# Cross-attention of a decoder step: three steps per token tile, sample queries spread by DMA, a sample's value products in four column groups

## The chip, the cores and the metric

The kernel runs on one core of a Trainium2 chip. The metric is the time of one execution on the device in microseconds; before the change the median of three runs is 2789.72 us (2788.94 to 2790.52).

## The reference

One layer of a decoder, in fp32, for a prompt of 1024 tokens and for 8 samples of one new token each: half-step SwiGLU, a token mixer (chunked gating beside an RWKV-7 scan), cross-attention into 256 memory tokens, half-step SwiGLU, final norm. The change is in the cross-attention alone:

```python
def cross_attn(h, mk, mv, w_q, w_o):
    bsz, t, _ = h.shape
    q = (h @ w_q).reshape(bsz, t, XA_HEADS, XA_HEAD_DIM)          # 4 heads of 256
    s = jnp.einsum('bthd,bmhd->bhtm', q, mk).astype(jnp.float32) * (XA_HEAD_DIM ** -0.5)
    p = jax.nn.softmax(s, axis=-1).astype(h.dtype)
    o = jnp.einsum('bhtm,bmhd->bthd', p, mv.astype(h.dtype)).reshape(bsz, t, D_MODEL)
    return (o @ w_o).astype(h.dtype)
```

The prompt has one memory (its keys and values are computed in the kernel). Each of the 8 samples has its own cached keys and values, 1 MB each, which are read from DRAM.

## The kernel before

Activations lie transposed in SBUF: x, qT and the like are [128, 8, 1032], with 1024 prompt tokens and the 8 samples as the last columns. Weights stream through four slots: SyncE loads raw pieces (line 335), GpSimd splits each into a high and a low part (lines 355 and 360), TensorE makes three products of a weight piece and 344 tokens (lines 382 to 384), and VectorE evacuates. All engines have their program written out by hand, and wait for one another by semaphores; what stands first in an engine's program is done first.

The attention lies between the projection xaq (it leaves qT) and the projection xao (it reads o_hi and o_lo, the two parts of the attention's output). `att_tensor`, `att_scalar` and `att_vector` hold the programs of TensorE, ScalarE and VectorE. Each goes through turns n = 0 to 8, with one tile of 128 prompt tokens each:

- scores of tile n into PSUM banks 0 and 1 (line 1739, n < 8); maxima (line 1877) and scaling (1880) on VectorE; exponentials with their sums on ScalarE (1826); reciprocal (1885) and normalisation (1886) on VectorE, into prob;
- in the next turn, for tile n - 1: eight transposes of prob into banks 2 and 3 (line 1760), copies to probT on ScalarE (1840), value products into banks 4 and 5 (1770), then o_hi on ScalarE (1845) and o_lo on VectorE (1914). On TensorE the value products stand right behind the transposes, and on ScalarE the copies to probT behind the exponentials of tile n.

The samples' work is threaded through the same turns. In turns 0 to 3, two samples each: TensorE spreads one query over all partitions by products of a broadcast column of qT with the identity (`att_query_pe`, line 1749, banks 6 and 7), and VectorE multiplies it with the sample's cached keys and sums, eight instructions a sample (`dots`, line 1863), into s_smp. In turn 4 the scores are transposed (1786), the sample softmax runs on 32 rows (1893 to 1898 and 1831), and the probabilities are transposed back (1795). In turn 5 they are spread into pT_smp, zero but for one sample's columns (1902 to 1905). In turns 5 to 8, two samples each: eight value products of 8 columns and 256 moving ones (line 1803), all writing rows 0 to 7 of banks 6 and 7. At the end o_rows is copied (1849 and 1919), transposed (1814), and becomes the last 8 columns of o_hi and o_lo (1851, 1921). The first product with xa_o waits for that.

SyncE's program holds, behind the weights of xaq, the loads of the 8 cached keys (`cache_loads`, line 1730) into two buffers, each behind the dot products that free its buffer, then those of the 8 cached values into the same two buffers, each behind the value products of the sample two before, then the weights of xao. GpSimd does nothing in the attention until the first piece of xa_o is there. An fp32 product shows in the trace as two records.

## Time and profile before

| | before |
|---|---|
| median of 3 runs | 2789.72 us |
| the profiled execution | 2790.14 us |
| its span (first to last instruction) | 2788.1 us |
| TensorE busy in the span | 2635.7 us (95%) |
| VectorE / ScalarE / GpSimd busy | 39% / 18% / 39% |
| attention, 1773.8 to 1921.7 us: TensorE / VectorE / ScalarE busy | 121.0 / 63.6 / 34.3 us of 147.9 |
| mean granted TensorE clock, whole span / attention | 0.965 / 0.91 of full speed |

A profile is one execution. Busy is the time in which an engine's instructions run; an idle engine costs time only where the chain that ended last passes through its wait. The granted clock is that of TensorE: 1.00 is 2.4 GHz and 0.50 is 1.2 GHz, and a value between them is a mean over a stretch with both. In a timeline, instructions of one line that follow one another are merged into one row with their count; the bracket gives the idle time of the engine before it and what released it.

### The profile page before, as it was taken

What the parts mean: (1) busy time and instruction counts of PE and PEld (TensorE: products, weight loads), DVE (VectorE), ACT (ScalarE), POOL (GpSimd) and SP (SyncE); (2) the same over time, 40 slices, a digit from 0 to 9 for tenths busy, and PEclk for the clock granted to TensorE, in tenths of its full rate; (3) what the DMA queues carried; (4) which work ended last, traced back from release to release, by engine and by line L of the source; (5) the groups of instructions that cost most, each with busy time, mean ns of one, the idle gap of its engine ahead of it and who ended that gap; (6) DMA issues with size and microseconds to landing.
All of it is one profiled execution on the core that took longest, in us unless ns stands there. A gap on an engine that the chain in (4) does not pass through costs nothing.

```text
span 2788.1 us, 50576 instructions
## 1 busy us (share of the span) xinstructions
PE 2635.7 (95%) x20619; PEld 2518.1 (90%) x20619; DVE 1086.5 (39%) x1850; ACT 515.0 (18%) x1035; POOL 1098.5 (39%) x866
## 2 busy tenths in 40 slices
PE   5999999999999998899978989879999999999998
PEld 5999999999999996789954989867999999999997
DVE  6332133223452674655445531442543213321333
ACT  4110011001221214322233240121211001100102
POOL 3444444444454441222214464002444444444442
PEclk8999999999999999899976999989999999999999
DMA  3111111111132110000023133123111111111111
GB/s 111 49 45 45 49 45 45 49 45 45 42 110 64 38 53 20 4 3 3 3 72 106 45 117 110 61 90 106 53 46 45 45 49 45 45 49 46 45 42 72
DMA packets 220704, 150.57 MB, mean 54 GB/s; under 512 B 10831, under 2 KB 211113, under 8 KB 219946
## 3 DMA queue, kind: packets, MB, share of 16 engines
q1 hardware_dynamic: 217530, 132.72, 15.9%
q10 hardware_dynamic: 2576, 16.11, 1.5%
q8 instruction: 89, 1.46, 0.2%
q14 instruction: 29, 0.24, 0.0%
q0 software_dynamic: 480, 0.05, 0.0%
HBM read 134.80 MB, written 14.04 MB: 53 GB/s over the span
## 4 chain that ended last, share of the span: by engine, by line
PE 92%; DVE 4%; ACT 2%; issue 1%; DMA 0%; POOL 0%; SPq 0%; DVEq 0%; ACTq 0%; POOLq 0%
PE bank L382 25%; PE bank L384 25%; PE bank L383 25%; PE bank L1020 1%; PE bank L1048 1%; PE bank L1770 1%; PE bank L1035 1%; PE bank L1739 1%; PE bank L1803 1%; PE bank L1064 1%; PE bank L1068 1%; PE bank L1089 1%; PE bank L1100 1%; PE bank L995 1%; PE bank L1079 1%
## 5 line engine op out<-in xcount | busy, mean ns | idle before, releaser
L355 POOL TENSOR_TENSOR w_hi<-raw,cst 128x512 fp32r<-128x512 f32 (+1 forms) x366 | 464.3, 1268 | 1238.7 <-PE bank L384 1067.5
L382 PE MATMUL bank<-h_hi,w_lo 128*128 128x344 f32 (+1 forms) x2856 | 915.3, 320 | 8.9 <-issue 7.5
L384 PE MATMUL bank<-h_hi,w_hi 128*128 128x344 f32 (+1 forms) x2856 | 913.1, 320 | 0.0
L383 PE MATMUL bank<-h_lo,w_hi 128*128 128x344 f32 (+1 forms) x2856 | 912.5, 319 | 0.0
L382 PEld LDWEIGHTS bank<-h_hi,w_lo 128*128 128x128 f32 (+1 forms) x2856 | 535.9, 188 | 11.2 <-issue 9.2
L360 POOL TENSOR_TENSOR w_lo<-raw,w_hi 128x512 fp32r<-128x512 f32 (+1 forms) x398 | 519.5, 1305 | 64.6 <-ACT w_hi L352 34.8
L384 PEld LDWEIGHTS bank<-h_hi,w_hi 128*128 128x128 f32 (+1 forms) x2856 | 536.1, 188 | 1.2
L383 PEld LDWEIGHTS bank<-h_lo,w_hi 128*128 128x128 f32 (+1 forms) x2856 | 534.9, 187 | 1.7
L384 PE MATMUL bank<-hid_hi,w_hi 128*128 128x344 f32 x1056 | 337.3, 319 | 0.0
L382 PE MATMUL bank<-hid_hi,w_lo 128*128 128x344 f32 x1056 | 337.2, 319 | 0.0
L383 PE MATMUL bank<-hid_lo,w_hi 128*128 128x344 f32 x1056 | 337.1, 319 | 0.0
L458 DVE TENSOR_TENSOR tmp<-bank,rstd 128x344 f32<-128x344 f32 x132 | 68.2, 517 | 338.2 <-PE bank L384 338.2
L492 DVE SCALAR_TENSOR_TENSOR x<-bank,x 128x344 f32 x120 | 62.0, 517 | 353.6 <-PE bank L384 353.6
L434 ACT ACTIVATE gate_s<-gate_s 128x344 f32<-128x344 f32 x132 | 64.6, 492 | 729.6 <-DVE gate_s L452 729.6
L384 PEld LDWEIGHTS bank<-hid_hi,w_hi 128*128 128x128 f32 x1056 | 198.6, 188 | 0.0
L382 PEld LDWEIGHTS bank<-hid_hi,w_lo 128*128 128x128 f32 x1056 | 198.5, 188 | 0.0
L383 PEld LDWEIGHTS bank<-hid_lo,w_hi 128*128 128x128 f32 x1056 | 198.2, 188 | 0.0
L452 DVE TENSOR_TENSOR gate_s<-bank,rstd 128x344 f32<-128x344 f32 x132 | 67.8, 516 | 289.9 <-PE bank L384 289.9
L438 ACT ACTIVATE hid_hi<-tmp 128x344 f32 (+1 forms) x132 | 64.9, 492 | 474.9 <-DVE tmp L464 474.9
L1273 POOL TENSOR_TENSOR LoT<-LQ,cst 128x512 f32<-128x512 f32 x40 | 51.7, 1301 | 168.7 <-PE bank L1020 87.2
L469 DVE TENSOR_TENSOR hid_lo<-tmp,hid_hi 128x344 f32 (+1 forms) x132 | 110.5, 863 | 0.0
L464 DVE TENSOR_TENSOR tmp<-tmp,gate_s 128x344 f32<-128x344 f32 x132 | 97.0, 735 | 13.8
(306 smaller groups left out, 3094.9 us busy)
## 6 DMA issues: line engine op xcount, KB each, us to landing
raw<-in_ffn_gate SPq DMA_DIRECT2D x88, 256.0 KB, 2.8
raw<-in_ffn_up SPq DMA_DIRECT2D x88, 256.0 KB, 2.9
raw<-in_ffn_down SPq DMA_DIRECT2D x80, 256.0 KB, 2.8
raw<-in_w_in SPq DMA_DIRECT2D x44, 256.0 KB, 2.8
cache<-in_cache_mem_k SPq DMA_DIRECT2D x8, 1024.0 KB, 5.0
cache<-in_cache_mem_v SPq DMA_DIRECT2D x8, 1024.0 KB, 4.9
x_save<-x ACTq DMA_DIRECT2D x1, 4128.0 KB, 12.5
x<-x_save ACTq DMA_DIRECT2D x8, 516.0 KB, 6.7
```

Of the source, the lines that this page charges most:

```text
L355: nc.gpsimd.tensor_tensor(w_hi[part], raw[part], cst[:, C_ONE:C_ONE + 1, 0:ph["width"]].to_broadcast([P, nk, ph["width"]]), ALU.mult)\
L360: nc.gpsimd.tensor_tensor(w_lo[part], raw[part], w_hi[part].bitcast(F), ALU.subtract).then_inc(split_done[slot], 1)
L382: nc.tensor.matmul(out, b, hi, start=first, stop=False)
L383: nc.tensor.matmul(out, a, lo, start=False, stop=False)
L384: m = nc.tensor.matmul(out, a, hi, start=False, stop=last)
L434: nc.scalar.activation(gate_s[:, t, :], gate_s[:, t, :], ACT.Silu)\
L438: nc.scalar.activation(hi[:, ds(i, 1), tslice(t)], tmp[:, t:t + 1, :], ACT.Copy).then_inc(S("hid_hi"), 1)
L452: nc.vector.tensor_tensor(gate_s[:, t, :], bank[3 * sg + t][:, 0:344], rstd[:, t, :], ALU.mult).then_inc(evac[sg], 1)
L458: nc.vector.tensor_tensor(tmp[:, t, :], bank[3 * su + t][:, 0:344], rstd[:, t, :], ALU.mult).then_inc(evac[su], 1)
L464: nc.vector.tensor_tensor(tmp[:, t, :], tmp[:, t, :], gate_s[:, t, :], ALU.mult)\
L469: nc.vector.tensor_tensor(lo[:, ds(i, 1), tslice(t)], tmp[:, t:t + 1, :], hi[:, ds(i, 1), tslice(t)].bitcast(F), ALU.subtract).then_inc(S( ...
L492: nc.vector.scalar_tensor_tensor(out=xs, in0=bank[3 * st + t][:, 0:344].rearrange("p (a n) -> p a n", a=1), scalar=scale, in1=xs, op0=ALU. ...
```

## The change

The turns become 0 to 9 and a tile goes through three of them instead of two. In turn n TensorE makes the scores of tile n, the transposes of tile n - 1 (`att_turn_pe`) and the value products of tile n - 2 (`att_out_pe`); ScalarE and VectorE follow (probT of tile n - 1, o_hi and o_lo of tile n - 2).

The queries of the samples are transposed once, ahead of turn 0, into 8 rows (`att_query_pe`), copied to q_rows, stored to a DRAM scratch q_d, and read back per sample to all 128 partitions (`query_loads` on SyncE's queue, between the key loads) into one of two buffers q_rep, behind the dot products that free it. The dot products read q_rep and not PSUM. They move to turns 1 to 4, the sample softmax to turn 5, the value products of the samples to turns 6 to 9.

The value products of a sample write head h into rows 32h to 32h + 7 of bank 6, with the head as the inner loop. The bank is set to zero before, o_rows is one copy of [128, 256], and two transposes replace eight. GpSimd waits for all dot products before it splits xa_o, since q_rows and q_rep lie in the buffers of the split weights.

```diff
@@ buffers
-        o_rows = at("o_rows", [NS, D], arena_z + 16 * ROW + 16384)
+        o_rows = at("o_rows", [P, XD], arena_z + 16 * ROW + 16384)
+        q_rows = at("q_rows", [NS, D], arena_w + 8192)
+        q_rep = [at("q_rep0", [P, D], arena_w + 16384), at("q_rep1", [P, D], arena_w + 20480)]
@@ TensorE
-        def att_query_pe(pe, n):
-
-            pe.wait_ge(S("s_dot"), 8 * n)
+        def att_query_pe(pe):
             for k in range(KD):
-                m = nc.tensor.matmul(bank[6 + k // 4][:, (k % 4) * P:(k % 4 + 1) * P],
-                                     qT[:, k, SEQ + n:SEQ + n + 1].to_broadcast([P, P]), ident,
-                                     start=True, stop=True)
-            m.then_inc(S("q_bc"), 1)
+                m = nc.tensor.transpose(bank[6 + k // 4][0:NS, (k % 4) * P:(k % 4 + 1) * P],
+                                        qT[:, k, SEQ:T], ident)
+                if k % 4 == 3:
+                    m.then_inc(S("srow"), 1)
+
+        def query_loads(sp, n):
+            if n == 0:
+                sp.wait_ge(S("rows_ev"), 2)
+                sp.dma_start(q_d, q_rows[:, :]).then_inc(S("scratch_stored"), 16)
+                sp.wait_ge(S("scratch_stored"), 32)
+            if n >= 2:
+                sp.wait_ge(S("s_dot"), 8 * (n - 1))
+            sp.dma_start(q_rep[n % 2][:, :], q_d[n, :].partition_broadcast(P)).then_inc(q_in[n % 2], 16)
...
+        def att_sample_pe(pe, b):
+            pe.wait_ge(S("srow_v"), 5)
+            pe.wait_ge(cache_in[b % 2], 64 + 16 * (b // 2 + 1))
+            for m in (0, 1):
+                for h in range(XH):
+                    i = nc.tensor.matmul(
+                        bank[6][32 * h:32 * h + NS, 0:XD],
+                        pT_smp[m].rearrange("p b x -> p (b x)")[:, 32 * b + 8 * h:32 * b + 8 * h + NS],
+                        cache[b % 2][:, m, h * XD:(h + 1) * XD],
+                        start=b == 0 and m == 0, stop=b == NS - 1 and m == 1, skip_group_check=True)
+            i.then_inc(S("o_smp"), 1)
...
-            for n in range(9):
+            att_query_pe(pe)
+            for n in range(10):
                 if n < 8:
                     att_scores_pe(pe, n)
-                if n < 4:
-                    att_query_pe(pe, 2 * n)
-                if n == 4:
+                if n == 5:
                     pe.wait_ge(S("s_dot"), 64)
...
-                if n:
-                    att_out_pe(pe, n - 1)
-                if n < 4:
-                    att_query_pe(pe, 2 * n + 1)
-                if n == 4:
+                if 0 < n < 9:
+                    att_turn_pe(pe, n - 1)
+                if n > 1:
+                    att_out_pe(pe, n - 2)
+                if n == 5:
                     pe.wait_ge(S("srow_v"), 2)
...
-                for b in (2 * n - 10, 2 * n - 9) if n > 4 else ():
...
+                if n > 5:
+                    att_sample_pe(pe, 2 * n - 12)
+                    att_sample_pe(pe, 2 * n - 11)
...
-            for k in range(KD):
-                i = nc.tensor.transpose(bank[0][:, k * NS:(k + 1) * NS], o_rows[:, k * P:(k + 1) * P],
-                                        ident[0:NS, 0:NS])
+            for d in (0, 1):
+                i = nc.tensor.transpose(bank[0][:, d * P:(d + 1) * P], o_rows[:, d * P:(d + 1) * P], ident)
             i.then_inc(S("srow"), 1)
@@ ScalarE
...
+                if n > 1:
+                    m = n - 2
+                    c = slice(m * P, (m + 1) * P)
                     for g in (0, 1):
                         act.wait_ge(S("pv"), 2 * m + g + 1)
@@ VectorE
-                dve.wait_ge(S("q_bc"), n + 1)
+                dve.wait_ge(q_in[b], 16 * (n // 2 + 1))
...
-                            in1=bank[6 + h // 2][:, (h % 2) * 256:(h % 2) * 256 + 256],
+                            in1=q_rep[b][:, h * XD:(h + 1) * XD],
...
-                    if n < 4:
-                        dots(2 * n)
+                    if 0 < n < 5:
+                        dots(2 * n - 2)
...
-                    if n < 4:
-                        dots(2 * n + 1)
+                    if 0 < n < 5:
+                        dots(2 * n - 1)
...
+                        nc.vector.memset(bank[6][:, 0:XD], 0.0).then_inc(S("srow_v"), 1)
@@ SyncE
             for n in range(8):
                 cache_loads(sp, "k", n)
+                if n == 1:
+                    query_loads(sp, 0)
+                if n > 0:
+                    query_loads(sp, n)
@@ GpSimd
+                if ph is xao:
+                    g.wait_ge(S("s_dot"), 64)
                 split_weights(g, ph, high=ph not in (memk, memv))
```

## Rows read from the trace of the kernel before

**Rows 1.** The page, part 4: the chain that ended last, by engine.
```profile
PE 92%; DVE 4%; ACT 2%; issue 1%; DMA 0%; POOL 0%; SPq 0%; DVEq 0%; ACTq 0%; POOLq 0%
```

**Rows 2.** Stretches: length, busy PE, PEld, DVE, ACT, POOL, then clock, DMA, GB/s.
```profile
1773.77:1921.67 147.90, 120.95 (x716) 96.65 (x717) 63.55 (x194) 34.25 (x100) 8.23 (x7) 0.91 0.33 111
...
1816.60:1832.90 16.30, 13.64 (x91) 12.67 (x90) 10.78 (x39) 4.10 (x12) 0.00 (x0) 0.90 0.38 129
```

**Rows 3.** Timeline of TensorE, turns with dot products: start, us, line, count [idle before].
```profile
1786.62 4.80 PE L1739 MATMUL bank<-kT,qT 128*128 128x256 f32 x16
...
1816.62 3.62 PE L1739 MATMUL bank<-kT,qT 128*128 128x256 f32 x16
...
1825.82 5.44 PE L1770 MATMUL bank<-probT,v_n 128*128 128x128 f32 x32 [2.35 <-ACT probT L1840]
1831.09 1.95 PE L1749 MATMUL bank<-cst,qT 128*128 128x128 f32 x16
```

**Rows 4.** Timeline of TensorE, turns with value products of samples, and the end.
```profile
1892.65 1.04 PE L1760 MATMUL bank<-cst,prob 128*128 128x128 f32 x8
1896.40 3.81 PE L1770 MATMUL bank<-probT,v_n 128*128 128x128 f32 x32 [2.71 <-ACT probT L1840]
...
1912.32 7.07 PE L1803 MATMUL bank<-cache,pT_smp 128*8 128x256 f32 x32
...
1921.67 0.42 PE L382 MATMUL bank<-o_hi,w_lo 128*128 128x344 f32 x1 [0.85 <-DVE o_lo L1921]
```

**Rows 5.** Timeline of VectorE at the end of turn 3 and in turn 4.
```profile
1833.08 0.42 DVE L1863 SCALAR_TENSOR_TENSOR s_junk<-cache,bank 128x256 f32<-128x256 f32 x1 [4.90 <-PE bank L1749]
...
1836.67 0.08 DVE L1863 DVE_READ_ACCUMULATOR s_junk<-cache,bank 128x1 f32 x1
...
1837.87 1.41 DVE L1877 TENSOR_REDUCE att<-bank 128x2 f32<-128x512 f32 x2
1839.31 0.17 DVE L1880 TENSOR_SCALAR att<-att 128x4 f32<-128x4 f32 x1
...
1841.69 1.22 DVE L1886 TENSOR_TENSOR prob<-prob,att 128x1024 f32<-128x1024 f32 x1
...
1844.22 0.34 DVE L1898 TENSOR_SCALAR p_smp<-p_smp,s_row 32x256 f32<-32x256 f32 x1
```

**Rows 6.** Timeline of ScalarE in turn 3: four exponentials, then the copies.
```profile
1823.26 0.47 ACT L1826 ACTIVATE prob<-bank,att 128x256 f32<-128x256 f32 x1 [7.63 <-DVE att L1880]
...
1825.07 1.09 ACT L1840 ACTIVATE probT<-bank 128x512 f32<-128x512 f32 x2
```

**Rows 7.** TensorE products in column groups and quadrants, and two weight loads (min/median/max).
```profile
914.54 1.09 PE L708 MATMUL bank<-gwT,vn 128*64 128x128 f32 x16
...
1158.12 1.91 PE L995 MATMUL bank<-AR,BK 64*64 64x128 f32 x61
...
L708 PEld LDWEIGHTS bank<-gwT,vn x128: 132/137/137, 914.5 to 1016.9; 128*64 128x64 f32 x128
...
L1803 PEld LDWEIGHTS bank<-cache,pT_smp x128: 85/90/90, 1862.4 to 1918.8; 128*8 128x8 f32 x128
```

**Rows 8.** Transfers: size, median us to landing; a wait for a store; a busy stretch.
```profile
cache<-in_cache_mem_k SPq DMA_DIRECT2D x8, 1024.0 KB, 5.0
...
fin_g<-in_final_norm SPq DMA_DIRECT2D x1, 512.0 KB, 4.9
...
SPq L1429 <- DMA smp_d<-smp_n: 7.2, 1, 7.2
...
1785.00:1787.00 2.00, 2.00 (x10) 1.95 (x10) 0.14 (x1) 0.00 (x0) 0.00 (x0) 0.50 1.03 426
```

**Rows 9.** Timelines of SyncE issues and of GpSimd at the end of the attention.
```profile
1903.79 3.82 SPq L1730 DMA_DIRECT2D cache<-in_cache_mem_v  x2
...
1913.20 1.26 POOL L355 TENSOR_TENSOR w_hi<-raw,cst 128x512 fp32r<-128x512 f32 x1 [160.02 <-DMA raw<-in_xa_o]
1914.54 1.27 POOL L360 TENSOR_TENSOR w_lo<-raw,w_hi 128x512 fp32r<-128x512 f32 x1
```

More of the change, by code:

```diff
@@ L1771, in att_out_pe @@
                                                  v_n[:, m, h * XD + d * P:h * XD + (d + 1) * P],
-                                                 probT[b][:, 2 * h + m, :], start=m == 0, stop=m == 1)
+                                                 probT[n % 2][:, 2 * h + m, :], start=m == 0, stop=m == 1)
                 i.then_inc(S("pv"), 1)
+        def att_sample_pe(pe, b):
[9 more added lines that the diff above has]
+            i.then_inc(S("o_smp"), 1)
         def att_tensor(pe):
@@ L1797, in att_tensor, with sample_cols @@
                     i.then_inc(S("srow"), 1)
-                for b in (2 * n - 10, 2 * n - 9) if n > 4 else ():
-                    pe.wait_ge(S("srow_v"), 4)
-                    pe.wait_ge(cache_in[b % 2], 64 + 16 * (b // 2 + 1))
-                    for h in range(XH):
-                        for m in (0, 1):
-                            i = nc.tensor.matmul(
-                                bank[6 + h // 2][0:NS, (h % 2) * XD:(h % 2 + 1) * XD],
-                                pT_smp[m].rearrange("p b x -> p (b x)")[
-                                    :, 32 * b + 8 * h:32 * b + 8 * h + NS], cache[b % 2][:, m, h * XD:(h + 1) * XD],
-                                start=b == 0 and m == 0 and h % 2 == 0, stop=b == NS - 1 and m == 1,
-                                skip_group_check=True)
-                    i.then_inc(S("o_smp"), 1)
-            pe.wait_ge(S("o_rows"), 2)
-            pe.wait_ge(S("o_hi"), 16)
+                if n > 5:
+                    att_sample_pe(pe, 2 * n - 12)
+                    att_sample_pe(pe, 2 * n - 11)
+            pe.wait_ge(S("rows_ev"), 3)
             pe.wait_ge(S("exp"), 32)
-            for k in range(KD):
-                i = nc.tensor.transpose(bank[0][:, k * NS:(k + 1) * NS], o_rows[:, k * P:(k + 1) * P],
-                                        ident[0:NS, 0:NS])
+            for d in (0, 1):
+                i = nc.tensor.transpose(bank[0][:, d * P:(d + 1) * P], o_rows[:, d * P:(d + 1) * P], ident)
             i.then_inc(S("srow"), 1)
+        def sample_cols():
+            return bank[0][:, 0:256].rearrange("p (d h x) -> p h d x", d=2, h=XH)[:, :, :, 0:NS]
         def att_scalar(act):
-            for n in range(9):
+            act.wait_ge(S("srow"), 1)
+            nc.scalar.activation(q_rows[:, 0:512], bank[6][0:NS, :], ACT.Copy).then_inc(S("rows_ev"), 1)
+            for n in range(10):
                 if n < 8:
@@ L1870, in att_vector @@
                 dve.wait_ge(evac[j], xaq["mm1"][j])
-            for n in range(9):
+            dve.wait_ge(S("srow"), 2)
+            nc.vector.tensor_copy(q_rows[:, 512:D], bank[7][0:NS, :]).then_inc(S("rows_ev"), 1)
+            for n in range(10):
                 if n < 8:
@@ L1917, in att_vector @@
                             .then_inc(S("o_lo"), 1)
-            dve.wait_ge(S("o_smp"), 8)
-            nc.vector.tensor_copy(o_rows[:, 512:D], bank[7][0:NS, :]).then_inc(S("o_rows"), 1)
+                if n == 5:
+                    dve.wait_ge(S("srow"), 4)
+                    for m in (0, 1):
+                        nc.vector.tensor_copy(
+                            pT_smp[m][:, :, 0:32:8],
+                            bank[7][:, m * 32:m * 32 + 32].rearrange("p (b h) -> p b h", b=NS))\
+                            .then_inc(S("srow_v"), 1)
             dve.wait_ge(S("o_hi"), 17)
-            nc.vector.tensor_tensor(o_lo[:, :, SEQ:T], bank[0][:, 0:64].rearrange("p (k b) -> p k b", k=KD),
-                                    o_hi[:, :, SEQ:T].bitcast(F), ALU.subtract).then_inc(S("o_lo"), 1)
+            nc.vector.tensor_tensor(o_lo[:, :, SEQ:T].rearrange("p (h d) b -> p h d b", d=2), sample_cols(),
+                                    o_hi[:, :, SEQ:T].rearrange("p (h d) b -> p h d b", d=2).bitcast(F),
+                                    ALU.subtract).then_inc(S("o_lo"), 1)
         def blk_rows(n):
@@ L1979, in program @@
         smp_d = nc.dram_tensor("smp_d", (6, NS, BW), F, kind="Internal").ap()
+        q_d = nc.dram_tensor("q_d", (NS, D), F, kind="Internal").ap()
         smp_od = nc.dram_tensor("smp_od", (NS, BW), F, kind="Internal").ap()
```

39 lines of the change are left out of this document (16 added, 23 removed).

## The prediction

> **What bounds the kernel now.** The chain of work that ended last comes first: 92% of it is TensorE [rows 1], so a change counts where TensorE stands idle, or where it stops doing work that is taken away. Next, the table of stretches cut where one token tile's turn of the attention ends and the next begins [rows 2], and in it the timelines of the three engines [rows 3 to 6]. The attention runs from 1773.8 us (behind the last piece of qT) to 1921.67 us (the first product with xa_o, [rows 2, 4]): 147.9 us, of which TensorE works 121, and in which the kernel makes nine turns. There are two kinds.
>
> Turns 0 to 3 each hold two samples' dot products on VectorE. A turn lasts 16.3 us with 13.6 us of TensorE and 10.8 us of VectorE [rows 2]: nobody is busy all the time, the engines wait for one another. TensorE spreads a query (1.95 us with its tail, [rows 3]), VectorE takes its products, the score products of the next tile stand behind the spread, and the value products wait 2.35 us for probT [rows 3], which ScalarE makes only after the exponentials of the same turn.
>
> Turns 5 to 8 each hold the value products of two samples: 32 records in 7.07 us, one every 221 ns [rows 4]. In turns 5 to 7 there is again a wait for probT, of 2.71 us [rows 4].
>
> **The change, part by part.** I lay the new order out turn by turn, with durations from the rows, first with TensorE at full clock and no late transfer.
>
> *Query spread.* It removes eight groups of 16 records from TensorE, about 1.8 us each beside their neighbours (1.95 less the tail), 14.4 us. It adds eight transposes of eight columns in their place, once, ahead of the first scores: eight transposes take 1.04 us with the tail [rows 4], so 1.0. The copies into q_rows hide behind the scores of tile 0. Then SyncE stores q_d, waits for it, and reads it back 128-fold, 512 KB a sample. Behind that wait on SyncE's queue stand only k loads 2 to 7, and these must wait for the first dot products anyway. The nearest row for a broadcast is fin_g, 512 KB landed in 4.9 us [rows 8]. A store followed by a wait took 7.2 us in a stretch full of other transfers [rows 8]; the trace has no quiet store of this size, so I take 2 with 7.2 as the other end. The rows of query 0 are there at 1775.7 + 2 + 4.9 = 1782.6, or 1787.8 at worst; they are wanted at 1785.8. Nothing to 2 us; I take nothing.
>
> *Turns 0 and 1.* Scores take 3.62 us [rows 3]. Turn 0: 1.0 + 3.6 of TensorE, 0.1 + 0.9 for the second maximum and the scaling (half of 1.41, and 0.17, [rows 5]), 1.9 for four exponentials (1823.26 to 1825.07, and a little to start them, [rows 6]): scores of tile 1 start at 1781.2, against 1786.6 now [rows 3]. VectorE has their maxima at 1785.8, then dot products 0, normalisation and dot products 1. Eight dot products take 3.6 us (1833.08 to 1836.67); a normalisation takes 1.22 [rows 5], with the small reciprocal before it 1.35. That ends at 1794.35. Reading the query from SBUF and not from PSUM I cost at nothing either way.
>
> *Turns 2 to 4* are VectorE's: 1.6 (maxima, scaling) + 3.6 + 1.35 + 3.6 + 1.2 (o_lo, 1836.67 to 1837.87) = 11.35 us [rows 5]. TensorE needs only 3.6 + 0.95 + 3.75 = 8.3 us of it (scores, transposes, value products, [rows 3, 4]) and its waits for exponentials and probT fall inside, since the value products now belong to the tile before. So three turns are 34.05 us: 1828.4.
>
> *Turn 5* has the sample softmax. From the first maximum to the end of p_smp the rows give 1837.87 to 1844.56, 6.7 us [rows 5]; with its transposes 1835.4. The memsets and o_lo lie behind that beside TensorE's 8.3 us of turn 6.
>
> *Samples' value products.* Now all four heads of a sample write 8 rows in a column group of their own. Products with two column groups, 16 records, took 1.09 us with a tail of 0.2, some 64 ns each, where 128 columns otherwise take about 117 ns (32 records in 3.75 us): 1.8 times as fast [rows 4, 7]. In four quadrants 64 records took 2.0 us, 32 ns each, 3.7 times [rows 7]. Four column groups are not in the trace. From both sides: 7.07 us a pair of samples if they don't overlap, 3.9 at the ratio of two groups, 1.9 at that of four quadrants. I take 2.0, since the number of tiles is that of the last row.
> The Trainium skill ("TensorE: Matmul & The Clock Gate", Part 3) says that a weight load overlaps a running product only where the row groups differ, and here all use the same 128 rows. The trace disagrees: with two column groups on the same rows a record came every 64 ns while a weight load lasts 137 [rows 7]. By that rule 32 loads of 90 ns would make 2.9 us a pair.
>
> *Turns 6 to 9.* Turns 6 and 7: 8.3 + 2.0 each, 1856.0. Turn 8 has no scores: 4.7, then sample 4. V load 5 was issued at 1856.0 behind v4. 1 MB lands in 5.0 us, and while it moves the transfers run at 426 GB/s [rows 8], 2.5 us each; so v5 lands at 1862.3, and sample 5 ends at 1863.3. There v7 is issued, right behind v6, and lands at 1869.0. Turn 9 does value products to 1867.1, sample 6 to 1868.1 and sample 7 to 1870.0. Now two things end together. The tail from the last sample product to xa_o takes 2.3 us today (1919.39 to 1921.67, [rows 4]): 1872.4. And xa_o's first piece, issued behind v7: it reaches GpSimd 6.0 us after v7's issue today (1907.24 to 1913.20), and the split takes 2.6 [rows 9]; v7 lands 5.7 us after issue here and 4.9 there, so 1872.8. This is what comes last: a new wait of 0.4 us that replaces a larger one, and GpSimd's added wait for the dot products is long fulfilled by then.
>
> **The sum.** 1921.67 - 1872.8 = 48.9 us. From it I take three costs. (a) The clock: after idle stretches the records show 1.2 GHz for some us; scores took 4.80 where 3.62 is usual, value products 5.44 for 3.81 [rows 3, 4]. Tile 1's scores come after 2.8 idle us: 1.2. The scores of tile 6 come after several short waits: 1.6. In turns 2 to 4 TensorE has 3 us to spare, so this costs nothing there. (b) Loads: k (2.5 us of moving), then the query (about 2.2, as 512 KB in smaller pieces), land some 7.3 us after dot products free the buffer; the next use comes 6.55 us later in turn 2, twice, and 7.75 later in turns 3 and 4. 1.5. Together 4.3, leaving 44.6. The profiled execution took 2790.14 (span 2788.1 and 2.0 around it), so 2745.5; the median of the runs is 0.4 lower. I say 2746.
>
> **Rivals.**
> *The column groups don't overlap* (the change does not do what it says). For: no row with four; all read the same partitions. Against: two groups gave 1.8. Each of four turns grows by 5.07, less 0.6 and 0.9 us of waits for loads and 0.4 at the end which vanish: +18.4, so 2764. With the ratio of two groups (3.9 a pair) it is about +6: 2752. With every weight load bare (2.9), +2.6: 2748.
> *TensorE at 1.2 GHz much of the time.* For: now it idles 3 of 11.35 us in turns 2 to 4; the granted clock is already 0.90 in a turn with 2.35 us of idle [rows 2, 3]. Against: behind the idle 2.71 us of turn 7 the value products took the usual 3.81 [rows 4], and the idle stretches of turns 6 to 9 go away. At a mean of 0.8 in turns 6 to 9 (some 34 us of products) and at the first scores: +8 or 9, 2755.
> *Loads bound turns 2 to 4.* A turn can't be shorter than landing time + 3.6. At 9.5 us from issue to landing it costs 2 x 2.95 us in turn 2 and 1.75 in each of the next two, 9.4 and so 7.9 more than under (b): 2754. **Slower than before** comes out by this mechanism only: three turns must lose 45 us, so the pair of loads must take about 15 us longer than the 7.75 that fit, some 23 us, three times my estimate, for example if the 128-fold read of one 4 KB row went through few engines. fin_g speaks against it. It would give 2795.
>
> **How the numbers follow.** My forecast, 2740 to 2753 with the milder overlap cases in it: 0.70. No overlap, 2764: 0.12. Clock, 2755: 0.09. Loads, 2754: 0.07. Slower: 0.02. The range runs from 2739 (nothing of (a) and (b) lost, and the better overlap) to 2765, which takes in no overlap. A difference of 0.2%, 5.6 us, is about what can be told from no change here; every case but the last is beyond it. Faster 0.97, same 0.01, slower 0.02.
>
> **What would show it.** Turns 2 to 4 of 11.4 us, VectorE busy over 90% in them; no wait of TensorE for probT; the sample's 16 records within 1.0 us (3.5 would be no overlap); about 3.6 us from one score group to the transposes and 8.3 + 2 in turns 6 and 7; xa_o's first product near 1877. I am wrong if VectorE's dot products wait for q_rep for more than 2 us in all, if the granted clock in turns 6 and 7 is below 0.9, or if anything after the attention changes its length by more than 2 us.

## The result, and the profile after

The changed kernel takes 2743.47 us (median of 4 runs, 2740.64 to 2744.99) beside 2789.33 for the kernel before on the same chip: ratio 0.9834, 95% interval 0.9819 to 0.985. The forecast was 2746, within 2739 to 2765. The profiled execution took 2743.82 us, its span is 2741.8.

Stretches of the kernel after: length, busy PE, PEld, DVE, ACT, POOL, granted clock, DMA share, GB/s. The first is the whole attention, from the query transposes to the first product with xa_o; then turns 2 to 4, cut where VectorE begins a turn's maxima; then turns 6 to 9, cut where TensorE begins a turn.

```profile
1773.98:1876.91 102.93, 80.71 (x591) 68.96 (x591) 63.46 (x195) 34.90 (x102) 2.58 (x3) 0.93 0.56 195
...
1796.40:1808.20 11.80, 6.25 (x39) 5.36 (x38) 10.82 (x41) 3.88 (x12) 0.00 (x0) 0.94 0.84 287
1808.20:1820.70 12.50, 10.61 (x56) 9.91 (x56) 10.88 (x40) 3.99 (x12) 0.00 (x0) 0.79 0.71 257
1820.70:1832.30 11.60, 8.35 (x54) 7.53 (x55) 10.84 (x40) 3.88 (x12) 0.00 (x0) 0.93 0.66 227
...
1839.30:1849.24 9.94, 9.94 (x90) 8.28 (x89) 6.22 (x13) 5.04 (x15) 0.00 (x0) 1.00 0.01 2
1849.24:1859.18 9.94, 9.94 (x92) 8.29 (x88) 4.31 (x7) 3.99 (x12) 0.00 (x0) 1.00 0.55 213
1859.18:1867.92 8.74, 6.70 (x76) 5.23 (x72) 1.38 (x2) 2.28 (x4) 0.00 (x0) 1.00 0.77 274
1867.92:1877.00 9.08, 6.40 (x71) 4.65 (x67) 1.61 (x3) 1.80 (x4) 2.67 (x3) 1.00 0.95 315
```

The attention takes 102.93 us instead of 147.90 [rows 2], 45.0 less. TensorE's busy time in it falls from 120.95 to 80.71, and its idle time only from 26.95 to 22.22. Of the 40.2 us of busy time, about 34 are work that is gone: four times 5.16 for the samples' products (7.07 less 1.91) and eight query spreads of about 1.8, less the 0.9 of the new transposes. The other 6 or so are products that ran at half clock before and no longer do. To credit the third step with the 4.7 us of idle time alone would be misleading (second experiment). Turns 2 to 4 are now VectorE's: it is busy 87 to 93% of them. Turns 6 and 7 are TensorE's without a gap, and turns 8 and 9 have waits again, with the DMA queues 77 and 95% busy.

TensorE's timeline of the kernel after (start, duration, line, records; in brackets the idle time before and what ended it), the rows where time is lost and one clean turn:

```profile
1781.48 5.41 PE L1742 MATMUL bank<-kT,qT 128*128 128x256 f32 x16 [3.01 <-ACT prob L1842]
...
1808.34 6.28 PE L1781 MATMUL bank<-probT,v_n 128*128 128x128 f32 x32 [3.72 <-DVE o_lo L1928]
...
1839.30 3.72 PE L1742 MATMUL bank<-kT,qT 128*128 128x256 f32 x16
1842.86 1.04 PE L1769 MATMUL bank<-cst,prob 128*128 128x128 f32 x8
1843.73 3.74 PE L1781 MATMUL bank<-probT,v_n 128*128 128x128 f32 x32
1847.40 1.91 PE L1791 MATMUL bank<-cache,pT_smp 128*8 128x256 f32 x32
...
1864.43 1.05 PE L1791 MATMUL bank<-cache,pT_smp 128*8 128x256 f32 x16 [0.58 <-DMA cache<-in_cache_mem_v]
1866.94 1.05 PE L1791 MATMUL bank<-cache,pT_smp 128*8 128x256 f32 x16 [1.46 <-DMA cache<-in_cache_mem_v]
...
1873.42 1.05 PE L1791 MATMUL bank<-cache,pT_smp 128*8 128x256 f32 x16 [0.68 <-DMA cache<-in_cache_mem_v]
1874.97 0.44 PE L1826 MATMUL bank<-cst,o_rows 128*128 128x128 f32 x2 [0.50 <-ACT o_rows L1867]
1876.91 0.42 PE L384 MATMUL bank<-o_hi,w_lo 128*128 128x344 f32 x1 [1.50 <-POOL w_lo L362]
```

The pair of samples that took 7.07 us [rows 4] takes 1.91 (1847.40). The scores at 1839.30 to the samples at 1847.40 are one turn without a wait: where turns 5 to 7 of before had 2.71 us for probT [rows 4], nothing is left. What is left: cold products, that is products at 1.2 GHz, after 3 us of idleness (1781.48: 5.41 where 3.72 is usual), 2.7 us of waits for value loads, and the last row, where xa_o's first product waits for GpSimd's split.

The remainder of the kernel changed too. The first 6 us from xa_o's first product on, of the kernel before and then of the kernel after:

```profile
1921.67:1927.67 6.00, 6.00 (x28) 6.00 (x29) 0.00 (x0) 0.00 (x0) 1.77 (x2) 0.72 0.30 90
```

```profile
1876.91:1882.91 6.00, 6.00 (x38) 6.00 (x39) 0.00 (x0) 0.00 (x0) 5.84 (x5) 1.00 0.31 90
```

In 6 us, 38 products instead of 28 run, at a granted clock of 1.00 instead of 0.72: 10 products of 0.16 us, 1.6 us. From xa_o's first product to the end the span is 866.4 us before (2788.1 less 1921.67) and 864.9 after, the same 1.5. Span before to span after: 45.0 in the attention, 1.5 behind it, less 0.2 by which the attention starts later, 46.3.

### The profile page after: what moved, and what is told of

The parts are those of the page before. It is cut to its first block, busy times and chain, and to the rows that moved or that the text cites. A ratio compares the mean times of both kernels' runs of the same rounds, so it can differ in the third digit from the quotient of the medians.

```text
span 2741.8 us, 50335 instructions
## 1 busy us (share of the span) xinstructions
PE 2595.5 (95%) x20493; PEld 2491.2 (91%) x20493; DVE 1084.8 (40%) x1851; ACT 514.3 (19%) x1036; POOL 1098.4 (40%) x866
## 4 chain that ended last, share of the span: by engine, by line
PE 89%; DVE 4%; issue 3%; ACT 2%; DMA 1%; POOL 0%; SPq 0%; DVEq 0%; ACTq 0%; POOLq 0%
PE bank L384 25%; PE bank L386 25%; PE bank L385 25%; PE bank L1022 2%; PE bank L1050 1%; PE bank L1037 1%; PE bank L1066 1%; PE bank L1070 1%; DMA q_rep<-q_d 1%; PE bank L1091 1%; DVE s_junk L1881 1%; PE bank L1102 1%; PE bank L997 1%; PE bank L1093 1%; PE bank L1081 1%
```

## The experiments

My theory is that of the prediction: each of the three parts does what it says, and what is left over is VectorE's work, loads and the clock. The rivals differ in how much each part carries. Each part is taken back alone first; then the groups are made alone. The kernel before took 2790.33 us on the chip of these four, 2789.33 beside the changed kernel and 2789.18 and 2789.35 on the chips of the later ones, so what an edit costs is the difference of two gains, each over the kernel before on its own chip; the change's gain is 45.9. By its 95% interval such a gain is good to some 4.5 us either way, so a difference of two gains from different chips to about 6.

**The column groups taken back.** All heads of a sample write rows 0 to 7 again; the transposes and the two copies of before come back with it.

```diff
-            for m in (0, 1):
-                for h in range(XH):
+            for h in range(XH):
+                for m in (0, 1):
                     i = nc.tensor.matmul(
-                        bank[6][32 * h:32 * h + NS, 0:XD],
+                        bank[6 + h // 2][0:NS, (h % 2) * XD:(h % 2 + 1) * XD],
```

> The changed kernel, but with the samples' value products as before: all four heads into rows 0 to 7 of banks 6 and 7, 32 records of 221 ns a pair of samples, and o_rows copied and transposed as before. My theory (the products of the four groups overlap, and they lie on TensorE's path in turns 6 to 9): each pair takes 7.07 us again for the 1.84 that it takes in the changed kernel, 20.9 in all, less the waits for value loads in turns 8 and 9 (0.6, 1.5 and 0.7 us) which vanish: +18, so 2762 us. Rival: the samples' products fill time in which TensorE would wait for loads anyway; then less than +6, under 2750.

Measured: 2762.1 us (2759.1 to 2762.26), ratio 0.9896 (0.988 to 0.9913). Its TensorE timeline, two of its four pairs:

```profile
1846.81 7.07 PE L1791 MATMUL bank<-cache,pT_smp 128*8 128x256 f32 x32
...
1884.29 7.07 PE L1791 MATMUL bank<-cache,pT_smp 128*8 128x256 f32 x32
```

A gain of 28.2 instead of 45.9: the groups are worth 17.7 us in the full kernel. Four times 5.16 would be 20.6; some comes back because none of these products waits for a load any more. The rival without overlap gave 2764, with +18.4. My own rival, that these products only fill time in which TensorE would wait for loads (under 2750), is out.

**The third step taken back.** The value products, o_hi and o_lo go back to the turn of the transposes; query spread by DMA and groups stay.

```diff
-                if n > 1:
-                    att_out_pe(pe, n - 2)
+                if 0 < n < 9:
+                    att_out_pe(pe, n - 1)
```

> The changed kernel, but in two steps a tile: the value products, o_hi and o_lo of tile n - 1 stand in turn n, right behind its transposes and its copies to probT. My theory: the wait for probT comes back, 2.7 us in each of turns 6 and 7, some 4 in turn 5 (there ScalarE also makes the exponentials of the samples first), under 1 in each of turns 2 to 4 where VectorE is the bound: +9 to +13, so about 2754 us. Rival: VectorE and the loads bound the turns and the wait hides: +3 or less, under 2747. Other rival: the third step is the main part of the gain of 46 us: +20 or more.

Measured: 2762.88 us (2761.61 to 2763.83), ratio 0.9903 (0.9886 to 0.9919), so the third step is worth 18.4 us (45.9 less 27.5). I had expected 2754, +9 to +13; the result is nearer to the rival with +20, in which this step is the main part. Rows of its TensorE timeline, one of turn 3 and then from turn 5 on:

```profile
1813.79 3.81 PE L1781 MATMUL bank<-probT,v_n 128*128 128x128 f32 x32 [2.71 <-ACT probT L1855]
...
1840.15 5.41 PE L1781 MATMUL bank<-probT,v_n 128*128 128x128 f32 x32 [5.04 <-ACT probT L1855]
...
1853.04 5.44 PE L1781 MATMUL bank<-probT,v_n 128*128 128x128 f32 x32 [2.71 <-ACT probT L1855]
1858.40 1.91 PE L1791 MATMUL bank<-cache,pT_smp 128*8 128x256 f32 x32
...
1867.55 5.36 PE L1781 MATMUL bank<-probT,v_n 128*128 128x128 f32 x32 [2.71 <-ACT probT L1855]
...
1886.05 1.90 PE L1791 MATMUL bank<-cache,pT_smp 128*8 128x256 f32 x16 [3.36 <-DMA cache<-in_cache_mem_v]
```

The wait of 2.71 us for probT is back, and in turns 6 and 7 the value products behind it take 5.4 us instead of 3.74: there a wait of 2.7 us costs 4.4. The wait alone does not decide this. In turns 1 and 3 of this kernel the same 2.71 us were followed by products of 3.81 us (1813.79), and in the kernel before by 3.81 in turns 5 and 7 [rows 4], but by 5.44 in turn 6:

```profile
1876.73 5.44 PE L1770 MATMUL bank<-probT,v_n 128*128 128x128 f32 x32 [2.71 <-ACT probT L1840]
```

From scores 6 to scores 7 it is 14.5 us (1845.73 to 1860.25) instead of 9.94. TensorE's busy time in the attention is 87.3 us here and 80.7 in the full change, for the same products: 6.6 us of it is clock, 10.2 us more is idle, and 2.2 more are lost behind the attention, where the clock is 0.59 in the first 6 us. So the 4.7 us by which idle time shrank from before to after is not what the third step is worth. Without it TensorE idles 32.4 us (119.71 of attention less 87.3), 5.4 more than before: that is what the other two parts uncover, and the third step takes 10.2 away.

**The query spread taken back.** The samples' queries are spread by TensorE's products into banks 6 and 7, with the dot products in turns 1 to 4.

```diff
+                if 0 < n < 5:
+                    att_query_pe(pe, 2 * n - 2)
...
+                if 0 < n < 5:
+                    att_query_pe(pe, 2 * n - 1)
...
-                            in1=q_rep[b][:, h * XD:(h + 1) * XD],
+                            in1=bank[6 + h // 2][:, (h % 2) * 256:(h % 2) * 256 + 256],
```

> The changed kernel, but with each query spread by TensorE's products into banks 6 and 7 as before, the first of a turn behind the scores and the second behind the value products; no q_d and no q_rep. My theory: in turns 1 to 4 VectorE is the bound at 11.35 us with or without them, TensorE has 8.3 + 3.6 = 11.9 us of work, VectorE waits some 0.6 us a turn for the second query, and the waits for q_rep (1.6 us) and the transposes ahead (0.9) go away: 2742 to 2746 us, no difference to the changed kernel. Rival: the products taken from TensorE (14.4 us) are time gained: +12 or more, over 2755.

Measured: 2752.16 us (2749.47 to 2752.91), ratio 0.9861 (0.9845 to 0.9878). The gain falls by 7.7 us (45.9 less 38.2), so this part carries something, against my expectation. Its TensorE timeline:

```profile
1790.34 3.42 PE L1751 MATMUL bank<-cst,qT 128*128 128x128 f32 x16 [2.89 <-DVE s_junk L1883]
...
1809.58 2.05 PE L1751 MATMUL bank<-cst,qT 128*128 128x128 f32 x16 [0.31 <-DVE s_junk L1883]
...
1841.71 0.42 PE L1821 MATMUL bank<-cst,p_smp 32*128 32x32 f32 x2 [2.78 <-DVE p_smp L1918]
1842.06 6.56 PE L1742 MATMUL bank<-kT,qT 128*128 128x256 f32 x16
```

The products themselves find room beside VectorE's turns. What costs is that each spread must wait until VectorE has read the one before out of the same banks, and VectorE then waits for the spread: 6.4 us in six waits, 2.16 the longest, where it waits 1.6 us for q_rep in the full change. And the scores of tile 6 run at half clock (6.56 us, +2.8), as do the first products with xa_o (granted clock 0.51 over 6 us, +2.7 us from there to the end). Against that, the scores of tile 1 ran at full clock here (3.72 us from 1781.07, where the change has 5.41), which gives 1.7 us back, and the transposes ahead are gone, 0.8. The span is 8.7 us longer than that of the change (2750.5 and 2741.8): 4.8 are the longer waits of VectorE (6.4 less 1.6), of which 1.4 are a spread at half clock (3.42 us at 1790.34 for 2.05), and some 3.8 net are the other places where the clock fell; the rest is a later start and value loads. So 4 to 5 us are clock. Whether these come with the edit, or with the moment, these runs don't separate: the changed kernel itself, profiled twice, has its cold value products in turn 3 once and in turn 4 the other time (1808.34 and 1820.98).

**The groups alone, on the kernel before.**

```diff
@@ on the kernel before
-                                bank[6 + h // 2][0:NS, (h % 2) * XD:(h % 2 + 1) * XD],
+                                bank[6][32 * h:32 * h + NS, 0:XD],
```

> The kernel before, with the column groups alone: the samples' value products, o_rows and its transposes as in the changed kernel, everything else (two steps, queries by products, turns 0 to 8) as before. My theory: turns 5 to 7 lose 5.2 us each, and the end (from sample 5 to xa_o) goes from 14.5 to 9 us, where the last loads bind: -21, so 2768 us. Rival: the freed time turns into waits for value loads and for probT, and half of it or less is gained: 2779 or more.

Measured: 2772.06 us (2769.64 to 2774.13), ratio 0.9932 (0.9916 to 0.9949), 18.3 us gained where I expected 21. Its TensorE timeline, of the slowest of the four runs:

```profile
1872.24 6.76 PE L1770 MATMUL bank<-probT,v_n 128*128 128x128 f32 x32 [2.71 <-ACT probT L1842]
1878.93 1.91 PE L1803 MATMUL bank<-cache,pT_smp 128*8 128x256 f32 x32
...
1888.09 5.44 PE L1770 MATMUL bank<-probT,v_n 128*128 128x128 f32 x32 [2.71 <-ACT probT L1842]
```

Here is the loss on TensorE that the taken-back third step showed: of the three value products behind 2.71 us, two run cold, 4.6 us together, where the kernel before had one (1.6 us). So 3.0 us of the four times 5.16 go to the clock. The three parts taken back one by one give 17.7 + 18.4 + 7.7 = 43.8, near the whole of 45.9. The groups are worth the same, within the noise, with the other two parts and without them (17.7 and 18.3), and the third step is worth 19.9 beside the groups alone (38.2 less 18.3) and 18.4 in the full kernel. So the gains in time nearly add up, although the idle times do not. The third step and the query spread alone, on the kernel before, were not run. Of the third step's worth 8.8 us are clock: 6.6 in the attention and 2.2 behind it.

**Two groups instead of four.** Heads 0 and 1 write one group, 2 and 3 another.

```diff
-                for h in range(XH):
-                    i = nc.tensor.matmul(
-                        bank[6][32 * h:32 * h + NS, 0:XD],
+                for hh in (0, 1):
+                    for g in (0, 1):
+                        h = 2 * g + hh
+                        i = nc.tensor.matmul(
+                            bank[6][32 * g:32 * g + NS, hh * XD:(hh + 1) * XD],
```

> The changed kernel, but the four heads in two column groups: heads 0 and 1 in rows 0 to 7, heads 2 and 3 in rows 32 to 39 of bank 6 (512 columns), in turns; o_rows and its transposes are twice as wide. If the rate goes with the number of groups, as in the kernel before with two groups of 64 columns: 110 to 120 ns a record, 3.6 to 3.9 us for two samples, +6 us to the changed kernel less 1 of waits for loads: 2749. If two groups are already as fast as four (one limit for all): 1.84 us a pair, no difference but 0.4 us at the end.

Measured: 2747.18 us in one run, too few for a verdict on the time; the pair takes 3.63 us. A row of its TensorE timeline:

```profile
1846.00 3.63 PE L1793 MATMUL bank<-cache,pT_smp 128*8 128x256 f32 x32
```

With one, two and four groups a record comes every 221, 113 and 60 ns (7.07, 3.63 and 1.91 us over 32). Two groups are 1.95 times as fast as one, four are 3.70 times.

**The order of the heads.** The four heads side by side, or a head's two halves behind one another (two records in the same group):

```diff
-            for m in (0, 1):
-                for h in range(XH):
+            for h in range(XH):
+                for m in (0, 1):
```

> The changed kernel, but the two products of a head (both halves of the memory) follow one another, so that four records in a row go to one column group. Theory A (each group has its own stream, a record starts as soon as its group is free): a waiting record holds up those behind it, so up to four records of 221 ns are in a row before the next group starts, and about two groups overlap at most: 16 records take 2 to 3.5 us where they take 0.92 now. Theory B (order doesn't matter, the records are queued by group): 0.92 us as now.

Measured: 2746.07 us in one run; a pair takes 1.93 us instead of 1.91. The order of the heads does nothing to the products, whose rows are what this run was for. Theory A had wanted 2 to 3.5 us for 16 records, and it is out (1.07 here). Of the mechanism, this says only that four groups are kept filled even when neighbours share one.

**A second transfer of each query.** SyncE loads every query twice, the second time into a weight slot that is free, and VectorE waits for both.

```diff
             sp.dma_start(q_rep[n % 2][:, :], q_d[n, :].partition_broadcast(P)).then_inc(q_in[n % 2], 16)
+            sp.dma_start(raw[:, 2 * (n % 2):2 * (n % 2) + 2, :, :].rearrange("p a b c -> p (a b c)"),
+                         q_d[n, :].partition_broadcast(P)).then_inc(q_in[n % 2], 16)
```

> The changed kernel, but every query is read from q_d a second time, 512 KB more a sample, into the idle raw weight buffers, and the dot products wait for both. My theory of the loads (a turn with two samples moves 2 x 2.5 us of keys and 2 x 2.2 us of queries through the 16 engines, against 11.4 to 12.5 us a turn): 13.8 us of moving a turn now bound turns 2 to 4, each by 2 to 2.5 us longer, and turn 2 more: +7 to +9, so 2752 us. Rival: the broadcast costs only latency, and twice the bytes are hidden: under +2.

Measured: 2746.71 us (2745.52 to 2748.03), ratio 0.985 (0.9833 to 0.9866), 3.4 us of the gain lost. That is within the noise of a difference between two chips, though each of its four runs is slower than each of the change's; the waits point the same way. What VectorE waits for, total, times and longest, in this kernel and then in the kernel after:

```profile
DVE s_junk L1883 <- DMA raw<-q_d: 4.3, 3, 2.8
```

```profile
DVE s_junk L1881 <- DMA q_rep<-q_d: 1.6, 4, 0.8
```

The wait grew by 2.7 us for 4 MB more (by 3.4 over the other profile of the change, with 0.9), so loads stand at the edge of setting turns 2 to 4: neither free (I had a rival under +2) nor the bound (+7 to 9). Each load landed 6.2 and 7.6 us after its issue, and the key loads beside them no later than before (4.9 us, against 6.1 and 5.2 in two profiles of the change). Landing times are no measure of the queue's room by themselves.

**The first idle stretch kept warm.** TensorE makes three useless products of 512 columns in its first 3 us wait; their results are never read.

```diff
+                if n == 0:
+                    pe.wait_ge(S("rows_ev"), 2)
+                    for _ in range(3):
+                        nc.tensor.matmul(bank[7][:, 0:512], kT[:, 0, 0:P], kT[:, 0:2, :].rearrange("p k n -> p (k n)"),
+                                         start=True, stop=True)
```

> The changed kernel with three products of 512 columns more, of no use, into the free bank 7 behind the scores of tile 0, where TensorE stands idle for 3.0 us; the output is the same. If the granted clock is what makes tile 1's scores 5.41 us and not 3.62: the idle stretch is filled, they take 3.6, and VectorE's turns start 1.8 us earlier: 2741.7 us. Rival: the scores are not on the path of turn 1 (VectorE would wait for the first query rows), or the clock falls all the same: no difference.

Measured: 2742.82 us (2740.83 to 2747.22), ratio 0.9833 (0.9817 to 0.985), no difference from the change that these runs can tell. Its TensorE timeline:

```profile
1779.61 2.74 PE L1808 MATMUL bank<-kT 128*128 128x512 f32 x6
1782.78 3.72 PE L1742 MATMUL bank<-kT,qT 128*128 128x256 f32 x16 [0.43 <-ACT prob L1847]
...
1789.51 5.41 PE L1742 MATMUL bank<-kT,qT 128*128 128x256 f32 x16 [2.13 <-ACT prob L1847]
...
1838.53 5.41 PE L1742 MATMUL bank<-kT,qT 128*128 128x256 f32 x16
```

This profile is of the slowest of the four runs, 4.4 us above their median. It does what was meant: the scores of tile 1 take 3.72 us instead of 5.41. VectorE's turn 2 begins 20.7 us after the attention's start (1796.02 less 1775.28), in the change 22.4 (1796.40 less 1773.98). The scores of tile 2 are now cold (1789.51, behind a wait of 2.13 that left the same scores warm in the change), but VectorE had other work until 1796.02, so they cost nothing. The 1.7 us are lost later: the scores of tile 6 (1838.53) are cold and were warm there, and the waits for value loads in turns 8 and 9 are 3.6 us instead of 2.7. The attention takes 103.46 us in this run, against 102.93. So in this run the gain was given back. How it went in the three faster runs no trace shows, and a gain of 1.8 us, as expected, is less than these medians could tell from none.

**The waits for loads removed.** Three edits of the transfers, none of the arithmetic. (1) Five q_rep buffers: SyncE spreads samples 0 to 4 right behind the store. (2) The values of samples 4 to 7 are loaded into the place of qT as soon as its last scores are done. (3) xa_o's first four pieces are loaded behind v1, and GpSimd splits them while the attention runs.

```diff
-            if n >= 2:
-                sp.wait_ge(S("s_dot"), 8 * (n - 1))
+            if n >= 5:
+                sp.wait_ge(S("s_dot"), 8 * (n - 4))
...
+            if name == "v" and n >= 4:
+                sp.wait_ge(S("score"), 16)
+                sp.wait_ge(S("s_dot"), 64)
+                sp.dma_start(cache_late[n - 4][:, :, :],
...
             for n in range(8):
                 cache_loads(sp, "v", n)
-            load_weights(sp, xao)
+                if n == 1:
+                    load_weights(sp, xao, 0)
+            load_weights(sp, xao, 1)
```

> The changed kernel with its loads moved, the arithmetic untouched. Five buffers for the spread queries in place of two (samples 0 to 4 are spread right behind the store, 5 to 7 behind k2 to k4); the value loads of samples 4 to 7 go to the place of the prompt's queries, which is free once the scores of tile 7 are done, and no longer wait for a buffer; the first four pieces of xa_o's weights are loaded behind v1, and GpSimd may split them at once. Theory A (after the change the path still holds waits for loads: 1.6 us on VectorE for the spread queries, 2.7 us on TensorE for v5 to v7, 1.5 us of xa_o's first product for the split): these 5.8 us go, less what the k loads lose because five spread queries now stand ahead of k2; 2738 to 2740. Theory B (the DMA queues are full in this stage, and what is loaded earlier only makes something else late): VectorE now waits for k2 and k3, 2743 or more. Warm clock after the attention as in the changed kernel.

**The changed kernel once more**, for the comparison on one chip:

> The changed kernel itself on the same chip as the two above, for their difference: 2743.5, within 0.1%.

**And the normalisation on ScalarE**, on top of the loads:

```diff
-                    nc.vector.tensor_tensor(prob[b][:, :, :], prob[b][:, :, :],
-                                            att[:, b, 2, :].unsqueeze(2).to_broadcast([P, XH, NMEM]),
-                                            ALU.mult).then_inc(S("pnorm"), 1)
@@ ScalarE
+                    for h in range(XH):
+                        nc.scalar.activation(prob[n % 2][:, h, :], prob[n % 2][:, h, :], ACT.Copy,
+                                             scale=att[:, n % 2, 2, h:h + 1]).then_inc(S("pnorm"), 1)
```

> e8_early_loads with one more edit: the probabilities are normalised on ScalarE (four copies with a scale, one for each head) in place of VectorE's one product of 128x1024, so that a turn of VectorE, which sets turns 1 to 4, is shorter by that product. If VectorE's own work sets the turns (its busy time 10.8 of 11.6 us in them), turns 1 to 4 lose about 1.2 us each, 4.8 in all: 2734 to 2736. If the landing of k loads already sets them (512 KB and 512 KB per 10.5 us is what the queues moved at 0.84 busy), VectorE waits for DMA instead and less than 2 us come: 2737 to 2740.

Measured in five runs each: the change again 2743.91 us (2742.6 to 2745.37); with the loads moved 2739.6 (2736.3 to 2740.97), ratio to the kernel before 0.9821 (0.9808 to 0.9834); with the normalisation as well 2733.72 (2733.55 to 2735.85), ratio 0.9803 (0.9789 to 0.9816). Every run of the last is below every run of the second, and these are below every run of the change on this chip. TensorE's timeline at the end of the attention, of the kernel with the loads moved:

```profile
1860.55 1.91 PE L1816 MATMUL bank<-cache_late,pT_smp 128*8 128x256 f32 x32
1862.39 3.84 PE L1802 MATMUL bank<-probT,v_n 128*128 128x128 f32 x32
1866.16 1.91 PE L1816 MATMUL bank<-cache_late,pT_smp 128*8 128x256 f32 x32
1868.58 0.44 PE L1851 MATMUL bank<-cst,o_rows 128*128 128x128 f32 x2 [0.50 <-ACT o_rows L1892]
1869.59 0.42 PE L397 MATMUL bank<-o_hi,w_lo 128*128 128x344 f32 x1 [0.57 <-DVE o_lo L1965]
```

No row waits for a DMA, and xa_o's first product waits 0.57 us for o_lo instead of 1.50 for GpSimd. Its attention takes 96.90 us (1772.69 to 1869.59) instead of 102.93, 6.0 less where 5.8 was the sum of the three waits. The medians say 4.3: the profiled run is the fastest of the five, 3.3 us under their median, so what it shows of the attention may be its best case.

With the normalisation moved, VectorE's turns 3, 4 and 5 begin at 1806.82, 1817.02 and 1827.22, 10.2 us apart, against 11.33 (1806.43, 1817.76, 1829.09) in the kernel with the loads alone: 1.1 us a turn for a product of 1.25. In turn 2 it waits once for a key load. What VectorE waits for in this kernel:

```profile
DVE s_junk L1911 <- DMA cache<-in_cache_mem_k: 1.4, 1, 1.4
```

So VectorE's own work did set the turns, and the loads are now the next bound. (What I wrote on loads before the run was miscounted: a turn moves two keys of 1 MB and two queries of 512 KB, not 1 MB in all.) The median is 5.9 us below the kernel with the loads moved, where 4.8 was expected, and 10.2 below the change. Against the change the profile says the same: an attention of 93.05 us (1773.90 to 1866.95), 9.9 less than 102.93.

## Why the prediction was right

**The sum.** The forecast for the profiled execution was 2745.5, with xa_o's first product at 1877.1 after the 4.3 us of costs. It came at 1876.91, with a start 0.2 us later. So the length of the attention was forecast to 0.4 us; the other 1.5 us lie behind it. Part of this closeness is luck: tile 6's scores began 1.0 us later than the forecast with its costs and the later start would have them (1838.3), and then the 1.6 us of clock that I put on these scores did not come. The figure of 2746 for the median was also rounded up: 2745.5 less 0.4 is 2745.1.

**Query spread: held.** The store was issued at 1775.86 and the first spread 1.8 us later; I took 2, with 7.2 as the other end. VectorE's first dot products did not wait. A dot product from SBUF takes 0.42 us, as from PSUM. The transfers ran beside VectorE's turns nearly as laid out, and taking this part back cost 7.7 us.

**Turns 0 and 1: right, cost (a) too small there.** Tile 1's scores began at 1781.48 (forecast 1781.2). They took 5.41 us: 1.8 lost to the clock, where I had 1.2. Turn 2 of VectorE began at 1796.40 instead of 1794.35, which is this and the later start.

**Turns 2 to 4: right.** 35.9 us to 1832.31, forecast 34.05 plus 1.5 of cost (b). VectorE waited 0.39, 0.82, 0.21 and 0.17 us for q_rep, 1.6 in all; with five buffers the turns are 11.33 us, where I had laid out 11.35. VectorE was busy over 90% only in two of the three turns, 87% in turn 3. That TensorE's cold products cost nothing there is right too: the value products at 1808.34 took 6.28 us, the clock was 0.79 in that turn, and its 1.6 us of VectorE's idle time hold 1.0 of wait for the loads, while the other 0.6 are there in turn 2 too.

**Turn 5: right but for cost (a).** From 1832.31 to tile 6's scores at 1839.30 it is 7.0 us, as forecast (1835.4 less 1828.4). The 1.6 us that I put on these scores for the clock did not come: 3.72 us. They did come in two experiments (6.56 and 5.41). The sum of both terms of (a) was 2.8, measured 1.8 in this run; where the cold stretch falls is not to be had from the profile of before, and it moves between two executions of the changed kernel too.

**Four groups: right by the row, wrong by the rule.** 1.91 us a pair, taken as 2.0 from the row of four quadrants [rows 7]. The groups of instructions of the kernel after, by line and shape, have the samples' products and their weight loads (busy time, mean ns of one, idle time before):

```profile
L1791 PE MATMUL bank<-cache,pT_smp 128*8 128x256 f32 x128 | 8.0, 379 | 2.7 <-DMA cache<-in_cache_mem_v 2.7
...
L1791 PEld LDWEIGHTS bank<-cache,pT_smp 128*8 128x8 f32 x128 | 3.0, 89 | 6.3 <-issue 3.8
```

A record takes 379 ns by itself, and one ends every 60. The 379 alone say little, since they are the same in the kernel before, where one ends every 221; it is the interval that shows several under way at once. The weight loads of 89 ns on the same 128 rows must then overlap products of other column groups, and one another. The Trainium skill ("TensorE: Matmul & The Clock Gate", Part 3) wants different row groups for that, and the trace disagrees here also with four groups. By that rule the estimate was 2.9 us a pair (32 loads of 90 ns). Another page of the Trainium skill, "TensorEngine Tiling (Array Packing)" ("When to Use Tiling"), gives column tiling a factor of four for a stationary side of 32 columns; here, with 8, 3.7 was measured (7.07 over 1.91), and 1.95 for two groups.

**Turns 6 to 9: two small misses that cancel.** Turns 6 and 7 took 9.94 us each, not 10.3. In turns 8 and 9, loads were waited for 0.58, 1.46 and 0.68 us, 2.7 in all; I had 0.6 and 0.9 for v5 and v7, and none for v4. The term mis-sized is the landing of the two value loads that follow one another: v4 took 5.8 us from its issue, where I had 5.0 [rows 8], and v5 7.5 where I had 6.3. The loads v6 and v7 took 4.9 and 5.2.

**The last wait: the right one.** I named GpSimd's split of xa_o's first piece as what comes last. The last row waits for it. With the pieces loaded earlier, the way from the last sample product to xa_o is 1.5 us instead of 2.4, so it cost 0.9 us and not 0.4.

**After the attention: missed.** I forecast no change there and got 1.5 us. Its cause is in the granted clock of xa_o's first 6 us, 0.72 before and 1.00 after. The experiments show the sign is not safe: it was 0.59 with two steps, 0.51 with the query by products and 0.72 with the warm products, and the time behind the attention follows it (867.1, 867.6 and 866.5 us against 864.9). So it does in all thirteen profiles: seven with 1.00 need 864.9 us there, four with 0.72 (the kernel before, one group, the groups alone, the warm products) 866.4 or 866.5. What decides the clock at that point stays open.

**The rivals.** No overlap was priced at 2764, and the kernel that has none took 2762.1. Loads as the bound of turns 2 to 4: a second query transfer cost 3.4 us, less than half of the 7 to 9 that it would cost if they were, so they were close but not there. The clock as a large loss did not happen: it was 1.00 in turns 6 to 9. But what I held against it was thin: I named the 3.81 us behind the wait of turn 7, and turn 6 of the same profile has 5.44 behind the same wait. The experiments make the clock the least understood term: of what the taken-back third step and query spread cost, 8.8 and 4 to 5 us were clock.

## What to carry to other kernels

Where several small products each fill a few columns of the array, put them into column groups of their own; the gain is nearly the number of groups. Do not price a part of a change by the net fall of an engine's idle time: work that is taken off an engine uncovers waits behind it, and an idle stretch of 2.7 us on TensorE cost 4.4 where the products behind it ran at half clock, as they did after some of these waits and not after others. A pipelining step that the idle times credit with 5 us was worth 18. Take each part back alone; here the gains so found nearly add up to the whole. When one bound falls, look for the loads that were issued late because nothing asked for them sooner: freed buffers and idle space moved them earlier, and this gave another 4.3 us.

## What was not expected of the hardware

- The granted clock fell and rose in different places from one kernel to the next, with nearly the same idle time in front. The same scores behind the same 2.13 us wait took 3.72 us in the change and 5.41 with the warm products. Two profiles of the changed kernel differ too: the value products of turn 3 took 6.28 us behind an idle 3.72 in one and 3.84 behind 3.47 in the other. Keeping one gap warm moved the loss in the profiled run and did not remove it.
- The spread of one 4 KB row from DRAM to 128 partitions (512 KB) landed in 5.7 to 6.6 us (medians of ten profiles) beside key loads of 1 MB with 4.9 to 6.1. Half the bytes are not faster. Doubling them over turns 2 to 4 raised what the queues moved (from 255 to 340 GB/s over the 37 us from 1796) and delayed the end by some 3.4 us only.
- Records of the same column group behind one another ran as fast as four groups in turn (1.93 and 1.91 us a pair). In these two orders the rate goes with the number of groups in the neighbourhood, and strict alternation is not needed.
